# Opening of a weight stage: two output tiles together over the contraction, sums of squares behind both, the spread inside the third tile

## The reference, cut to what matters

```python
def rmsnorm(x, g):
    xf = x.astype(jnp.float32)
    y = xf * lax.rsqrt(jnp.mean(xf * xf, axis=-1, keepdims=True) + EPS)
    return (y * g.astype(jnp.float32)).astype(x.dtype)
...
    h = h + 0.5 * swiglu(rmsnorm(h, ffn1_norm[i]), ffn1_wg[i], ffn1_wu[i], ffn1_wd[i])
    a = rmsnorm(h, mix_norm[i])
    u = a @ w_in[i]
...
    h = h + 0.5 * swiglu(rmsnorm(h, ffn2_norm[i]), ffn2_wg[i], ffn2_wu[i], ffn2_wd[i])
    gate = jax.nn.sigmoid(rmsnorm(h, ple_gate_norm[i]) @ ple_w_gate[i])
    e = rmsnorm(p[i] @ ple_w_proj[i], ple_norm[i])
    h = h + gate * e
...
    u = rmsnorm_2(h, attn_norm_w)
    proj = u @ w_in
...
    u2 = rmsnorm_2(h, ffn_norm_w)
    a, val = jnp.split(u2 @ w_up, 2, axis=-1)
```

## Time and profile before

| | |
|---|---|
| runs | 2428.23, 2431.22, 2437.74 us; median 2431.22 us |
| profiled execution | 2435.61 us, of which the span is 2433.8 us |
| PE busy | 2293.5 us, 94% of the span |
| PE weight loads | 1987.8 us, beside the matmuls |
| DVE, ACT, POOL busy | 866.7, 794.9, 829.6 us |
| DMA | 179.51 MB, 74 GB/s mean |

### The profile page before, as it was taken

One profiled execution on the slowest core, in us unless ns is written; L12 is line 12 of the kernel. 1 busy time (PEld: TensorE's weight loads), 2 busy tenths in 40 slices (PEclk: granted clock), 3 DMA queues, 4 the chain that ended last, 5 costly groups with the idle time before them and its releaser, 6 DMA issues.

```text
span 2433.8 us, 33664 instructions
## 1 busy us (share of the span) xinstructions
PE 2293.5 (94%) x13205; PEld 1987.8 (82%) x13205; DVE 866.7 (36%) x1290; ACT 794.9 (33%) x1120; POOL 829.6 (34%) x229
## 2 busy tenths in 40 slices
PE   6999999998798889999999899999988899999997
PEld 5888887776687678888787899999987689998886
DVE  4222103103555452222105712243139336556401
ACT  4434313122565544343314432211100323433311
POOL 2434443430202234334333233344323203433432
PEclk8999999987888899999999999999998879999999
DMA  4232322340000022233232222222210002223231
GB/s 144 90 100 90 104 86 86 93 142 19 1 2 1 1 78 86 88 101 98 75 104 70 70 94 94 90 86 86 87 53 1 18 1 88 86 86 103 87 103 61
DMA packets 150737, 179.51 MB, mean 74 GB/s; under 512 B 6925, under 2 KB 140398, under 8 KB 150654
## 3 DMA queue, kind: packets, MB, share of 16 engines
q1 hardware_dynamic: 150491, 178.35, 22.6%
q10 hardware_dynamic: 163, 0.04, 0.0%
HBM read 176.28 MB, written 2.10 MB: 73 GB/s over the span
## 4 chain that ended last, share of the span: by engine, by line
PE 69%; issue 16%; DVE 8%; POOL 4%; ACT 2%; SPq 1%; DMA 0%; DVEq 0%; POOLq 0%; ACTq 0%
PE ps L1498 42%; PE ps L1624 10%; POOL wlo L602 4%; PE ps L1906 2%; PE ps L1847 2%; PE ps L1817 2%; DVE Ad L1408 1%; PE ps L1829 1%; DVE Q L1425 1%; PE ps L1572 1%; PE ps L1743 1%; PE ps L1714 1%; DVE eT L1290 1%; PE ps L1732 1%; PE ps L1815 1%
## 5 line engine op out<-in xcount | busy, mean ns | idle before, releaser
L602 POOL TENSOR_TENSOR wlo<-raw,whi 128x2048 fp32r<-128x2048 f32 x160 | 737.7, 4611 | 1279.6 <-ACT whi L671 1279.6
L1498 PE MATMUL ps<-xh,whi 128*128 128x512 f32 (+2 forms) x2432 | 700.4, 334 | 12.8 <-DVE xl L1000 6.0
L1498 PE MATMUL ps<-xh,wlo 128*128 128x512 f32 (+2 forms) x2432 | 701.5, 334 | 0.0
L1498 PE MATMUL ps<-xl,whi 128*128 128x512 f32 (+2 forms) x2432 | 700.3, 334 | 0.0
L671 ACT ACTIVATE whi<-raw 128x2048 fp32r<-128x2048 f32 x160 | 305.0, 1906 | 759.4 <-PE ps L1498 445.4
L1498 PEld LDWEIGHTS ps<-xh,whi 128*128 128x128 f32 x2432 | 417.8, 190 | 63.2 <-DVE xl L1000 6.5
L1498 PEld LDWEIGHTS ps<-xl,whi 128*128 128x128 f32 x2432 | 416.1, 190 | 46.0
L1498 PEld LDWEIGHTS ps<-xh,wlo 128*128 128x128 f32 x2432 | 414.8, 190 | 46.2
L1624 PE MATMUL ps<-act_l,whi 128*128 (+1 forms) x528 | 208.6, 395 | 0.0
L1624 PE MATMUL ps<-act_h,wlo 128*128 (+1 forms) x528 | 208.6, 395 | 0.0
L1624 PE MATMUL ps<-act_h,whi 128*128 (+1 forms) x528 | 208.6, 395 | 0.0
(11 more groups left out here) (305 smaller groups left out, 2731.9 us busy)
## 6 DMA issues: line engine op xcount, KB each, us to landing
raw<-in_w_in SPq DMA_DIRECT2D x47, 1024.0 KB, 5.0
raw<-in_ffn_wg SPq DMA_DIRECT2D x22, 1024.0 KB, 5.3
raw<-in_ffn_wu SPq DMA_DIRECT2D x22, 1024.0 KB, 5.3
raw<-in_ffn_wd SPq DMA_DIRECT2D x22, 1024.0 KB, 4.9
raw<-in_w_up SPq DMA_DIRECT2D x22, 1024.0 KB, 5.1
raw<-in_w_down SPq DMA_DIRECT2D x11, 1024.0 KB, 4.9
raw<-in_w_out SPq DMA_DIRECT2D x8, 1024.0 KB, 5.1
raw<-in_ple_w_gate SPq DMA_DIRECT2D x4, 1024.0 KB, 5.1
```

The source lines that it names most:

```text
L602: nc.gpsimd.tensor_tensor(wlo[:, slot, 0:n], raw[:, slot, 0:n], whi[:, slot, 0:n].bitcast(F32), ALU.subtract).then_inc(lo_ready, 1)
L1498: last = mm(ps[:, j * banks + b, 0:n], w[:, k, e * P:(e + 1) * P], x[:, k, c0:c0 + n], start=(k == 0 and q == 0), stop=(k == KD - 1 and q ...
```

## The change

`opening` now takes the contraction step outside and the two tiles inside, with `free(e)` asked at the first step of tile e. The sums come behind both tiles. Tile 2 follows at once, and the spread stands before its fifth contraction step (k = 4). Tile 3 is as before. Since tile 2 can now write bank 5 while the sums are still read, `SSQ` moves to bank 7, and the transposes of the start move from bank 7 to bank 4. In W_PLG the two spreads change places, since one of them goes to bank 7.

```diff
-        SSQ, RB = 5, 6
+        SSQ, RB = 7, 6
...
                 pe.wait_ge(lo_ready, u + 1)
-                for e in range(2):
-                    free(e)
-                    for k in range(KD):
-                        if e == 0:
-                            pe.wait_ge(xl_ready, KD * v + k + 1)
+                for k in range(KD):
+                    pe.wait_ge(xl_ready, KD * v + k + 1)
+                    for e in range(2):
+                        if k == 0:
+                            free(e)
                         last = products(e, e, p, xs, splits[0], banks, k)
-                        if e and k == 5:
-                            sums()
-                    last.then_inc(tiles_done, 1)
-                spreads()
+                        if k == KD - 1:
+                            last.then_inc(tiles_done, 1)
+                sums()
                 pe.wait_ge(lo_ready, u + 2)
-                for e in range(2):
-                    if e and kept is not None:
-                        pe.wait_ge(*kept)
-                    tile_mm(2 + e, e, 1 - p, xs, splits[1], banks)
+                for k in range(KD):
+                    if k == 4:
+                        spreads()
+                    last = products(2, 0, 1 - p, xs, splits[1], banks, k)
+                last.then_inc(tiles_done, 1)
+                if kept is not None:
+                    pe.wait_ge(*kept)
+                tile_mm(3, 1, 1 - p, xs, splits[1], banks)
...
-                nc.tensor.transpose(ps[:, 7, t * P:t * P + NROWS[t]], rows_t[0:NROWS[t], t, :], ident[0:NROWS[t], 0:NROWS[t]]).then_inc(colsT, 1)
+                nc.tensor.transpose(ps[:, 4, t * P:t * P + NROWS[t]], rows_t[0:NROWS[t], t, :], ident[0:NROWS[t], 0:NROWS[t]]).then_inc(colsT, 1)
...
             def both_spreads():
+                norm_spread(4, True)
                 norm_spread(3, True, 8, 7)
-                norm_spread(4, True)
```

More of the change, by code:

```diff
@@ L747, in _ @@
             for t in (1, 2):
-                nc.scalar.activation(cols[:, t, 0:NROWS[t]], ps[:, 7, t * P:t * P + NROWS[t]], ACT.Copy).then_inc(cols_ready, 1)
+                nc.scalar.activation(cols[:, t, 0:NROWS[t]], ps[:, 4, t * P:t * P + NROWS[t]], ACT.Copy).then_inc(cols_ready, 1)
             act.wait_ge(metaT, 1)
-            nc.scalar.activation(h[:, :, 0:M], ps[:, 7, 0:KD * M].rearrange("p (n m) -> p n m", n=KD), ACT.Copy).then_inc(meta_ready, 1)
+            nc.scalar.activation(h[:, :, 0:M], ps[:, 4, 0:KD * M].rearrange("p (n m) -> p n m", n=KD), ACT.Copy).then_inc(meta_ready, 1)
             root(0, 1)
@@ L1679, in _ @@
             for n in range(KD):
-                last = nc.tensor.transpose(ps[:, 7, n * M:(n + 1) * M], meta_tok[:, n * P:(n + 1) * P], ident[0:M, 0:M])
+                last = nc.tensor.transpose(ps[:, 4, n * M:(n + 1) * M], meta_tok[:, n * P:(n + 1) * P], ident[0:M, 0:M])
             last.then_inc(metaT, 1)
```

## The result

Fifteen executions of each kernel on one chip gave a median of 2439.67 us for the changed kernel (2435.12 to 2447.18) against 2433.48 us for the one before (2428.23 to 2437.74). The ratio is 1.0031 with a 95% interval of 1.0019 to 1.0042: slower, by little, but more than the uncertainty. The forecast of 2429.5 us had the wrong sign, and its range ended at 2436.5. The mean clock that TensorE was granted fell from 0.951 to 0.947 in the profiled executions (2435.61 and 2439.67 us).

What follows compares the result with a forecast made beforehand. PE, busy 94% of the span, was taken as the bound, so order gains only where PE waits or runs at the lower clock. −1.4 + 0 − 0.3 = −1.7 us from the median 2431.2 gave 2429.5 us, range 2424 to 2436.5.

Steps and rivals of the forecast that it cites:

- W_IN1: Opening of W_IN1: six matmuls run inside the 5.83 us wait ahead of the sums, 4.4 us left; −1.4 us.
- rival A: The clock stays up after the waits left in W_IN1 and W_PLG: 2424.6 us if both; chance 20%.
- W_UP2 and W_UP3: Openings of W_UP2 and W_UP3: no wait to shorten and no idle PE ahead of tile 4; 0 us.
- W_PLG: Opening of W_PLG: wait 5.08 to 3.7 us, POOL's step earlier, first L1290 not held, DVE's chain 0.5 us earlier.
- W_IN2: Opening of W_IN2: one wait of nearly 8 us for tile 1's banks, then 15 steps left; −0.3 us.
- Rival B: W_IN2's long wait costs: low clock over all 15 steps, 2435.8 us, or mostly absent there before; chance 15%.
- Rival C: DVE meets POOL elsewhere: one more held L1290 in W_PLG's chain gives 2433.5 us, one less 2425.5; chance 10%.
- the sum: Whole kernel: −1.4 (W_IN1) + 0 − 0.3 (W_IN2) = −1.7 us, taken off the whole time to give 2429.5 us.
- rival D: Nothing comes through: PE's gain at W_IN1 is taken back at a later wait another chain sets, 2431.2 us; chance 5%.

Runs made afterwards that it cites:

- e6: New opening in W_UP2 and W_UP3 alone, old opening in the other stages, with the change's bank numbers: ratio 0.9996 to the kernel before.
- e8: Changed kernel with the old nest in all five openings (tile 0 over its eight steps, then tile 1): ratio 1.0021 to the kernel before.
- e9: Changed kernel plus five matmuls of 512 columns (1.2 us) ahead of tile 3 of W_IN1: ratio 1.0001 to the kernel before.
- e11: Old openings everywhere with the change's bank numbers, plus ten matmuls (2.3 us) ahead of tile 3 of W_IN1: ratio 1.0030 to the kernel before.
- e13: Changed kernel with the old opening in W_IN2, plus five matmuls (1.2 us) ahead of tile 3 of W_IN1: ratio 0.9992 to the kernel before.
- e1: Old openings everywhere, with only the change's new bank numbers and new order of W_PLG's two spreads: ratio 0.9994 to the kernel before.
- e10: Old openings everywhere with the change's bank numbers, plus five matmuls (1.2 us) ahead of tile 3 of W_IN1: ratio 1.0010 to the kernel before.
- e12: Changed kernel plus ten matmuls of 264 columns (1.2 us) ahead of tile 3 of W_IN2: ratio 1.0022 to the kernel before.
- e14: Changed kernel plus five matmuls ahead of tile 3 of W_IN1 and five of 512 columns ahead of tile 3 of W_IN2: ratio 1.0017 to before.
- e7: New opening in W_PLG alone, old opening in the other stages, with the change's bank numbers: ratio 0.9998 to the kernel before.
- e4: New opening in W_IN2 alone, old opening in the other stages, with the change's bank numbers: ratio 1.0008 to the kernel before.

## Why the prediction was wrong

**The steps on the openings held.** W_IN1: the wait came out at 4.52 us (4.4), the gain at 0.9 us in the profiled execution and at 1.4 over the traces of all kernels (1.4 forecast); the low clock came all the same, so rival A, the clock stays up, did not occur. W_UP2 and W_UP3: no wait for tile 4, and e6 measured even, though the trace has 0.2 us more in W_UP3 where I had 0. W_PLG: the wait, POOL's earlier step and the free L1290 as forecast, `rbs` 0.5 us later than I had it, so DVE's chain was 0.2 us later and not 0.5 earlier. W_IN2: one wait of 7.64 us for DVE's `gateT`, even with before up to tile 2 where I had -0.3. Rival B, the low clock over all 15 steps behind that wait, did not occur: the first 5.7 us had a clock of 0.65, and behind 7.64 us of waiting the tiles took 1380.64 - 1367.80 = 12.8 us, where 13.3 were forecast. Nor did its other condition hold, that the clock mostly stays up there before: it falls to 0.50 in W_IN2's opening in all nine traces with the old one there. Nor did the nest by itself show a price: with the old nest back, e8, the ratio was 1.0021 against 1.0031 and 1.0028, no difference beyond the uncertainty. Rival C did not occur either: two L1290 were held behind the first tile, for 4.70 and 4.69 us, as before.

**The step that failed is the sum.** I wrote "-1.4 + 0 - 0.3 = -1.7 us" and subtracted it from the whole time, as if everything behind an opening kept its length and only came earlier; the stages behind stood in the sum at nothing, without a reason. In the profiled executions they were not nothing: C grew by 1.7 us, S by 1.1 and V by 0.6, in code that the change doesn't touch, and the stretch from W_UP2 to 1187 us by 1.4, of which e6 shows nothing for the new opening in it. That is where theory L fails, and e9, e11 and e13 refute it: a stage that comes about 1 us earlier or later can itself become 2 us shorter or 10 us longer (C from 163.9 to 162.1 in e9, from 162.1 in e1 to 172.0 in e10). The prediction's nearest thought was rival D, "what PE gains is taken back at a later wait"; it bounded the take-back by the gain. Here more was taken than had been won.

**The row that I passed over** is on my own list: in W_IN2 a pair of matmuls took 0.48 us behind a wait of 1.35 and 0.81 behind others. I used the low clock as a price that goes with a wait. I did not ask whether it also depends on when the wait comes, nor look at the stages behind, where PE works in small matmuls between waits and the mean clock is 0.67 to 0.78 over 20 us (594 to 614 above). I also took the 5.6 and 5.7 us of the earlier trace rows for the length of the low clock, and called them alike; they are the lengths of the stretches that I had cut out. The low clock lasted at least 6.7 us in W_IN1 and 9.9 in W_IN2, as the rows in the first section show.

**The base and the range.** I set the profiled execution off by 4.4 us against a median of three runs. Of before's 15 executions the median was 2433.48, so 2.3 us of the miss of 10.2 are there; 1.7 are the forecast gain that isn't in the time, and 6.2 the loss that is. And the range, 2424 to 2436.5, was made of local mechanisms; the spread between executions of one kernel, 5 to 20 us in these runs, was not in it.

**What stays open.** The table of the twenty traces says where the fall stands when a stage is long; which waits and matmuls of the stage make it so isn't known, and I could not place a stage beforehand with certainty: V came as expected in two of the last three kernels and not in e12 and e14, C in e11 and e13 and not in e10. Why the kernel before so seldom shows a long execution is known in part: e7, whose program is that of before up to 1300 us, had C at 170.7, but S and V were 3.9 and 1.7 us shorter than in before, and the execution took 2436.41 us. A rival for the padding isn't excluded by a run of its own: the added matmuls also move the instructions behind them in the program, and in e12 and e14 such a thing slowed a loop. Against it for C stands that the lengths sort by the clock's fall in kernels with and without padding alike. And e13's advantage over before, 0.0008, is within its interval: it has the lowest ratio, with 1.2 us of added work in it, and isn't shown to beat the kernel before.

## What to carry to other kernels

Where PE's clock falls and rises inside a kernel, as it does here, a change that moves later stages by about a microsecond need not be worth that microsecond: the stages behind may change by several, in both directions. Test it by adding a known delay at the same place; if time doesn't follow the delay, a difference of a few tenths of a per cent between two orders says nothing on the orders. And such a kernel has to be compared over a dozen executions with their clock, never by one profile against another.

## What the runs showed of the hardware

Two kernels with one program up to there, six microseconds at the same place: clock 1.00 and 82 matmuls, or 0.50 and 30 (e1 and e4). Adding 1.2 us of matmuls made a kernel 0.3% faster (changed and e9). Levels of the same work took 162.2 us with the clock's fall 0.8 us behind their start and 166.1 with it 3.4 us behind (e13 and e9).

DVE's L1290 took 0.69 us with POOL's L602 finished, and 4.71 beside it; POOL's step there, before:

```profile
1334.55 4.63 POOL L602 TENSOR_TENSOR wlo<-raw,whi 128x2048 fp32r<-128x2048 f32 x1 [8.82 <-ACT whi L671]
```

In W_PLG POOL's step came 2.5 us nearer to the sums (4.17 us behind their start instead of 6.72), and one L1290 was freed, as forecast.

Five or ten matmuls added in W_IN2's opening made the loop behind it run at 820 instead of 824 matmuls in 100 us at full clock, 1.8 us over the loop. The same number added in W_IN1 did not. No run here explains it.
